# A decoder step on one core: the last expert's weights fetched early into used-up buffers, and the normed rows kept in DRAM

## What is computed

```python
h2 = rmsnorm(x, g_norm_ffn) * (1.0 + scale_f) + shift_f
gates = sigmoid_topk_gates(hb, w_router, b_router)      # 64 experts, top 8 per token
a = einsum('td,edf->tef', hb, w_e_gate)                 # d = 1024, f = 256
b = einsum('td,edf->tef', hb, w_e_up)
routed = einsum('tef,efd->td', silu(a) * b * gates[..., None], w_e_down)
shared = (silu(hb @ w_sh_gate) * (hb @ w_sh_up)) @ w_sh_down
x = x + gate_f * (routed + shared)
```

## Time and profile before

| | us |
|---|---|
| median of three runs | 1048.29 |
| lowest and highest | 1045.4, 1052.0 |
| the profiled execution | 1046.96 |
| its span, first to last instruction | 1045.2 |
| PE busy in the span | 1012.8 (97%) |
| DVE, ACT, POOL busy | 400.3, 219.3, 56.6 |

### The profile page before, as it was taken

One profiled execution on the slowest core, in us unless ns is written; L12 is line 12 of the kernel. 1 busy time (PEld: TensorE's weight loads), 2 busy tenths in 40 slices (PEclk: granted clock), 3 DMA queues, 4 the chain that ended last, 5 costly groups with the idle time before them and its releaser, 6 DMA issues.

```text
span 1045.2 us, 14232 instructions
## 1 busy us (share of the span) xinstructions
PE 1012.8 (97%) x4798; PEld 574.9 (55%) x4798; DVE 400.3 (38%) x1082; ACT 219.3 (21%) x443; POOL 56.6 (5%) x81
## 2 busy tenths in 40 slices
PE   7999999899999999999999999999999999999997
PEld 2477856444447788877644444444444444444443
DVE  2603212558754011123643343343333433433434
ACT  3311222335435100002411111111111111111110
POOL 0100001000000000000210000000000000000000
PEclk9999999999999999999999999999999999999999
DMA  8994478755545752553368999999999999999981
GB/s 316 418 367 174 169 235 290 184 159 159 153 120 228 296 208 100 202 201 132 155 241 333 415 410 418 419 413 411 408 426 418 419 420 415 413 405 424 415 356 44
DMA packets 53330, 310.67 MB, mean 297 GB/s; under 512 B 8746, under 2 KB 28234, under 8 KB 31778
## 3 DMA queue, kind: packets, MB, share of 16 engines
q1 hardware_dynamic: 46962, 296.13, 72.2%
q0 software_dynamic: 6320, 13.93, 3.7%
HBM read 315.80 MB, written 2.87 MB: 305 GB/s over the span
## 4 chain that ended last, share of the span: by engine, by line
PE 93%; DVE 3%; issue 1%; ACT 1%; DMA 1%; SPq 0%; DVEq 0%; POOLq 0%; ACTq 0%
PE bank L686 54%; PE pA L686 21%; PE pB L686 6%; PE pC L686 5%; PE bank L1218 3%; PE bank L1244 1%; PE pD L686 1%; PE pA L721 1%; PE pA L929 0%; DVE rstd L1712 0%; PE pC L938 0%; DMA xs<-h_rows,idx 0%; DVE xT L2287 0%; DVE hT L2095 0%; DVE hT L1740 0%
## 5 line engine op out<-in xcount | busy, mean ns | idle before, releaser
L686 PE MATMUL pA<-ring,qT 128*64 128x512 f32 x1008 | 226.7, 595 | 0.0
L686 PE MATMUL bank<-hT,ring 128*128 128x264 f32 (+1 forms) x832 | 192.0, 390 | 1.0 <-PE bank L686 1.0
L686 PEld LDWEIGHTS bank<-hT,ring 128*128 128x128 f32 (+1 forms) x832 | 156.8, 190 | 35.1 <-issue 8.0
L686 PEld LDWEIGHTS pA<-ring,qT 128*64 128x64 f32 x1008 | 70.7, 137 | 129.5 <-issue 129.5
L686 PE MATMUL bank<-pT,vtok 128*128 128x264 f32 x512 | 127.7, 393 | 0.9 <-ACT vtok L1641 0.9
L686 PEld LDWEIGHTS bank<-pT,vtok 128*128 128x128 f32 x512 | 92.2, 190 | 39.6 <-issue 26.9
L2216 DVE TENSOR_TENSOR pT<-pT,bank 128x264 f32<-128x264 f32 x248 | 99.4, 427 | 8.5 <-PE bank L686 6.9
L2239 DVE SCALAR_TENSOR_TENSOR oaT<-oaT,sinT,pA 128x256 f32<-128x256 f32 x32 | 15.4, 481 | 214.6 <-ACT oaT L1637 214.6
L686 PE MATMUL bank<-wuk,ring 128*128 128x512 f32 x192 | 86.6, 599 | 0.0
L686 PE MATMUL pB<-ring,oaT 128*64 128x512 f32 x252 | 62.0, 605 | 0.0
L686 PE MATMUL pC<-ring,oaT 128*64 128x512 f32 x252 | 60.4, 592 | 0.0
(11 more groups left out here) (318 smaller groups left out, 826.4 us busy)
## 6 DMA issues: line engine op xcount, KB each, us to landing
ring<-in_w_e_gu SPq DMA_DIRECT2D x63, 2048.0 KB, 10.2
ring<-in_w_e_dn SPq DMA_DIRECT2D x63, 1024.0 KB, 10.9
ring<-in_poolT SPq DMA_DIRECT2D x64, 208.0 KB, 2.7
ring<-in_w_ada SPq DMA_DIRECT2D x12, 1024.0 KB, 7.6
ring<-in_w_bg SPq DMA_DIRECT2D x4, 3072.0 KB, 10.3
ring<-in_w_mix SPq DMA_DIRECT2D x5, 2048.0 KB, 8.7
ring<-in_w_ada SPq DMA_DIRECT2D x4, 2048.0 KB, 12.5
ring<-in_poolR SPq DMA_DIRECT2D x56, 128.0 KB, 2.3
```

Source lines behind the costliest of these rows:

```text
L686: return nc.tensor.matmul(out, lhsT, rhs, start=start, stop=stop)
```

## The change

The gate, up and down weights of expert 63 (`LAST`) are no longer loaded by `refill(29)` into the ring. They are loaded once into buffers that are free by then. `h2tok` takes k-tiles 0 to 5 of the gate and up weights, the first part of `hT` the other two. The first half of the down weights goes into the second part of `hT`, and the rest into `wrou` and `bsp`. SP does this between expert 3 and expert 4: it waits for `h2s` and `h2`, stores `hT` in a new DRAM tensor `h2kept` for the general path, waits for that store, for the six stores of `d_tok` and for bank `shup1`, and then issues five loads of 3,072 KB together. PE waits for `d_last` before the last pair. The general path first reads `h2kept` back into `hT`. Apart from that, the identity's load at the start counts on `d_late` instead of a semaphore of its own.

```diff
-LOADS = [[place(e)[0] for e in range(1, E)].count(b) for b in range(NSLOT)]
+LAST = E - 1
+LOADS = [[place(e)[0] for e in range(1, LAST)].count(b) for b in range(NSLOT)]
...
+        hTf, h2f = hT[:].rearrange("p k t -> p (k t)"), h2tok.rearrange("p j c -> p (j c)")
+        wrf, bsf = wrou[:].rearrange("p k e -> p (k e)"), bsp[:].rearrange("p k t -> p (k t)")
+        last_gu = [h2f[:, k * 512:(k + 1) * 512] for k in range(6)] + [hTf[:, k * 512:(k + 1) * 512] for k in range(2)]
+        last_dn = [[hTf[:, (2 + hf) * 512:(3 + hf) * 512] for hf in range(2)], [wrf, bsf]]
...
+        h2kept = nc.dram_tensor("h2_kept", (P, DT, NT), F32, kind="Internal").ap()
...
-            for b, e in ((3, 3), (2, 4)):
-                reuse(b, "exp")
-                routed(b, e)
+            reuse(3, "exp")
+            routed(3, 3)
+            sp.wait_ge(s["h2s"], 1)
+            sp.wait_ge(s["h2"], DT)
+            sp.dma_start(h2kept, hT[:]).then_inc(d_last, 16)
+            sp.wait_ge(d_last, 16)
+            sp.wait_ge(d_tok, 16 * 6)
+            n = BASE["shup1"]
+            sp.wait_ge(full[n % 4], n // 4 + 1)
+            sp.dma_start(h2f, A["w_e_gu"][LAST][:, 0:6].rearrange("p k c -> p (k c)")).then_inc(d_last, 16)
+            sp.dma_start(hTf[:, 0:1024], A["w_e_gu"][LAST][:, 6:8].rearrange("p k c -> p (k c)")).then_inc(d_last, 16)
+            sp.dma_start(hTf[:, 1024:2048], A["w_e_dn"][LAST][:, 0]).then_inc(d_last, 16)
+            sp.dma_start(wrf, A["w_e_dn"][LAST][:, 1, 0:512]).then_inc(d_last, 16)
+            sp.dma_start(bsf, A["w_e_dn"][LAST][:, 1, 512:D]).then_inc(d_last, 16)
+            reuse(2, "exp")
+            routed(2, 4)
...
-            refill(29, None, (62, 63))
+            refill(29, None, (62,))
...
             with sp.If(over >= 1):
                 sp.wait_ge(s["dn1"], NPAIR)
+                sp.dma_start(hT[:], h2kept).then_inc(d_last, 16)
...
-            pool.dma_start(ident[:], A["ident"]).then_inc(d_fold, 16)
+            pool.dma_start(ident[:], A["ident"]).then_inc(d_late, 16)
...
-            pe.wait_ge(d_fold, 16)
+            pe.wait_ge(d_late, 16)
...
                     if e == 0:
                         pe.wait_ge(d_first, 16 * 4)
                         gu.append(first_gu)
+                    elif e == LAST and i is None:
+                        pe.wait_ge(d_last, 16 * 6)
+                        gu.append(last_gu)
...
                     if e == 0:
                         dn.append(first_dn)
+                    elif e == LAST and i is None:
+                        dn.append(last_dn)
...
             with pe.If(over >= 1):
                 pe.wait_ge(s["fgates"], 1)
+                pe.wait_ge(d_last, 16 * 7)
```

More of the change, by code:

```diff
@@ L348, in build @@
         d_early = [sem(f"early_pages{g}") for g in range(len(EGROUP) - 1)]
-        d_fold = sem("identity_input")
         d_c = sem("conditioning")
@@ L353, in build @@
         d_first = sem("first_expert")
+        d_last = sem("rows_kept_last_expert")
         d_tabs = sem("routing_tables")
@@ L596, in _ @@
             pool.dma_start(zs[:, 0:2], A["stateT"]).then_inc(d_late, 16)
-            pool.wait_ge(d_late, 16 * 7)
+            pool.wait_ge(d_late, 16 * 8)
             pool.wait_ge(s["ckv"], 1)
@@ L797, in _ @@
             colsum("kvn", sq[:, QT + KT_ + 1, :], 3)
-            pe.wait_ge(d_late, 16 * 7)
+            pe.wait_ge(d_late, 16 * 8)
             ada_item(4)
@@ L1763, in _ @@
             dve.sem_inc(s["varlat"], 1)
-            dve.wait_ge(d_late, 16 * 7)
+            dve.wait_ge(d_late, 16 * 8)
             dve.wait_ge(s["krin"], 1)
```

## The result

The changed kernel takes 1054.66 us (median of 14 runs, 1050.84 to 1057.63), the kernel before 1048.55 us in the runs beside them. The ratio is 1.0053, with a 95% interval of 1.0035 to 1.0071. So the change makes the kernel slower by about 5.6 us, within the 1% that were called the same. The profiled execution took 1057.48 us, near the upper end of its runs, and its span is 10.6 us longer than that of before. The first task is therefore to divide up these 10.6 us, and not to take all of them for the change.

The account below looks back on a forecast made before the run. PE was taken to set the pace, with transfers only looking full. Terms 0 + 0 + 0 + 5.0 gave 5.0 us, on the 1048.3 median 1053.3 (profiled execution: 1046.96 to 1052.0); range 1046.5 to 1058.5.

Parts of the forecast that it names:

- The mechanism: At the expert stage's start, the first two gathers land late beside the moved load, by 2.9 to 5.4 us; chance 0.62.
- The timing of the moved load: Between experts 3 and 4: `hT` stored by 512, five loads from 522.2, over by 524.3, landed about 533.
- SP's waits: Before the five loads: `shup1` decides at 522.2, expert 4 isn't issued before 530.74, so nothing is held up; cost 0.
- The size of the term: PE's first two gather transposes: 2.9 and 5.0 us late, the second covering the first; price 5.0 us.
- The step that I left as a condition: At the second gather: the load goes on past it, expert 4 following without a gap; 5.0 us, otherwise 2.9.
- The clock: At PE's waits for the gathers: a possible fall to 1.2 GHz costing 1.7 to 3.4 us, only in the range.
- The Trainium skill's rule: At the first two gathers: queues alternate packet by packet, half rate, each 1.3 us later, sum 1.3 us.
- the removed load: Expert 63 in refill 29: 10.6 us of slack, gives 0; rival of 7.6 us back, chance 0.06.
- the store: `hT`, 1.08 MB, before the moved loads: 6 us at most, landed by 512, hidden; cost 0.
- the third gather: After the first transpose: moves to 538, lands at 546.8, wanted at 546.6 + 5.0, so hidden.
- the backlog: Behind expert 63's load: at most 7.6 us, gone before the loaded stage; rival slower by over 1%, chance 0.07.

Follow-up runs that it names:

- e1: Changed kernel, but SP waits for the first two gathers before issuing expert 63's five loads, and so expert 4's too: 1050.34 us, ratio 1.0004.
- e2: Changed kernel with the three loads that don't write `hT` issued ahead of the wait for bank `shup1`: 1050.22 us, ratio 0.9995.
- e6: Changed kernel, but SP waits for the first two gathers before issuing expert 4's loads; expert 63's stay put: 1051.27 us, ratio 1.0024.
- e3: Changed kernel without the store of `hT` in `h2kept`, SP's wait for it and its reading back: 1054.54 us, ratio 1.0047.
- b3: Kernel before, with unread products filling PE's waits before the position counts (4) and before `a_transpose(0)` (5): 1044.93 us, ratio 0.9961.
- c1: Changed kernel with two thirds of expert 63's load ahead of the `shup1` wait, and PE's gates and `a_transpose(0)` waits filled: 1045.06 us, ratio 0.9962.
- b2: Kernel before with expert 63's load left out, the last pair using expert 59's weights: 1048.96 us, ratio 1.0004.

## Why the prediction was right

**The mechanism** was the one forecast. The price comes from two gathers that share the queues with the moved load. PE waits for them, and all later work moves with it. Taking the overlap away in two ways, later (e1) and earlier (e2), takes the loss away.

**The timing of the moved load** held. The store was issued at 505.80 and landed after 3.9 us (forecast: near 506, 6 us at most). The five loads were issued 0.1 us after the end of `shup1`, and expert 4 0.1 us after `shared_down`. SP's waits held up nothing.

**The size of the term** was 5.0 us for the gathers and measured 4.5. The first was forecast at 8.4 us and took 7.3, so PE reached it 1.9 us late and not 2.9. The second took 7.9 and not 8.4. The step that I left as a condition, that the load goes on past the second gather through expert 4, proved to be the larger half (e6: without it 1.96 us in all).

**The clock** is the term that I priced rightly and placed wrongly. I gave 1.7 to 3.4 us and measured 2.7, but I left it out of the sum. Both profiles with two full waits show the fall, and e3's puts its price at 1.8 us. With it the sum would have been 7.7, against a measured 7.2 in the profile and 5.6 by the ratio. That the sum of 5.0 comes so near to 5.6 is in part luck: the gathers were put 0.5 us too high, and the clock, at 0, too low by what it costs in the median run, which no run shows. I had also compared only the waits that the change makes. The existing wait for the gates has the same fall in 6 of the 9 profiles in which it isn't filled, before and after alike, at 3.3 us in the profile of the changed kernel. It is probably a part of the scatter of the runs: with this wait and the one near 206 filled, b3's and c1's runs lie within 3.2 us each, those of before beside them within 7.2.

**The Trainium skill's rule** on turns between queues ("DMA: Bandwidth & Descriptors", section "Queues, rings and completion order") was taken in the prediction to mean half the rate, at 1.3 us for each gather. The runs have 2.8 and 4.5 us in the changed kernel. The 0.56 MB of that estimate are too many as well. They count all 128 slots, and only slots that hold a token are fetched: from 560 to 960 us the DMA view of before has 7.34 MB in POOL's queue for 25 gathers, 0.29 MB each (which is also what makes 6.6 MB of a gather and two experts), and from 525 to 534.3 it has 0.52 MB for the first two. At 417 GB/s half the rate then costs an estimated 0.6 to 0.7 us, still further from the runs. Turns by packet are turns by bytes only between packets of one size, and here they aren't: from 560 to 960 us POOL's queue moved 3,600 packets of 2.0 KB on average, SP's 14,507 of 10.9 KB. So the runs refute the half rate. Whether packets of unequal size explain the landings no run here tests. That the gathers aren't simply queued behind everything else does agree: the first of them landed at 536.0, before the last of expert 63's loads (527.54 + 10.1 = 537.6).

**What was said to be 0** was 0: the removed load (b2), the store (e3), the third gather (issued at 539.67, landed at 546.2, wanted at 557.1) and the backlog (e1, twice as large there).

## What to carry to other kernels

A load that is moved into an idle stretch of the queues is free only if the small transfers issued there have slack: look for the DMA on which the chain of waits hangs, not at the share of the queues. A gather of 0.26 to 0.29 MB needs 3.4 to 4.6 us in free queues and 7 to 9 beside a stream of weights, and if its consumer waits on the spot, all of the difference reaches the end. A wait of PE that can't be removed can be filled with unread products, but they must be sized from a whole product's time and end before the wait does.

## What the runs showed of the hardware

The clock can fall at waits of PE of 2 to 3 us. Before `a_transpose(0)` the kernel before has two waits close together, 3.2 us of idle time around 0.66 us of work:
```profile
205.29 0.66 PE L929 MATMUL pA<-ident,pT 128*128 128x128 f32 x4 [0.72 <-ACT pT L1482]
...
208.45 0.90 PE L938 MATMUL pC<-ident,abuf 128*128 128x128 f32 x3 [2.50 <-DVE abuf L1965]
```
In every one of the 10 profiles in which the longer wait is left as it is, the granted clock fell to 1.2 GHz there. In none of the two in which it was filled did it fall there. Behind the single wait of 2.4 us for the gates it fell in 6 of 9, and in none of 3 when filled. Why the same wait has a fall in one execution and not in another stays open. Filling the two is worth 4 us of 1,049 (ratio 0.9961). The clock also fell near 190 us in 5 of the 12 profiles and near 355 us in 9, at places where no run filled a wait. In its section "Part 1: The HAM clock gate" the Trainium skill's page "TensorE: Matmul & The Clock Gate" says that the clock follows how busy the engine has lately been. These runs agree.
